# Three pairs of groups instead of two in each feed-forward stage of a two-block transformer kernel

## What is computed

```
def swiglu_ffn(h, w_gate, w_up, w_down):
    return (jax.nn.silu(h @ w_gate) * (h @ w_up)) @ w_down

for layer in range(DEPTH):          # DEPTH = 2
    ...
    h = rmsnorm(x, norm_ffn_g[layer])
    x = x + swiglu_ffn(h, ffn_w_gate[layer], ffn_w_up[layer], ffn_w_down[layer])
```

## Time and profile before

| | |
|---|---|
| median of 3 runs | 716.3 us (716.2 to 716.61) |
| the profiled execution's own time | 715.99 us |
| its span, first to last instruction | 714.1 us |
| TensorE matmul busy | 701.0 us, 98% |
| VectorE busy | 586.1 us, 82% |
| ScalarE busy | 422.6 us, 59% |
| granted TensorE clock, mean | 0.993 of full |

### The profile page before, as it was taken

The page is one execution under the profiler, slowest core; times in us unless marked ns, Lnnn a source line. Parts: engine busy times, 40 slices in busy tenths (PEclk is TensorE's granted clock), DMA queues, the critical chain, the costliest instruction groups (busy, mean ns, idle before and its releaser), DMA issues.

```text
span 714.1 us, 9602 instructions
## 1 busy us (share of the span) xinstructions
PE 701.0 (98%) x3764; PEld 609.7 (85%) x3764; DVE 586.1 (82%) x879; ACT 422.6 (59%) x640; POOL 12.4 (2%) x18
## 2 busy tenths in 40 slices
PE   7999999999999999999999999999999999999996
PEld 6888889989999999888788888888888888888885
DVE  5879999798976889988889688875698896888744
ACT  3156535974775768778845546364667455463623
POOL 0000000000220001000000000000000000000000
PEclk8999999999999999999999999999999999999998
DMA  8999996499935338534704860776345047607501
GB/s 333 417 421 417 422 405 268 175 378 345 391 119 212 145 128 264 138 119 177 265 31 148 324 235 1 307 282 235 119 178 214 22 156 315 236 0 295 176 1 60
DMA packets 23469, 158.41 MB, mean 222 GB/s; under 512 B 2624, under 2 KB 2880, under 8 KB 5248
## 3 DMA queue, kind: packets, MB, share of 16 engines
q1 hardware_dynamic: 22464, 152.82, 55.4%
q0 software_dynamic: 960, 4.98, 2.6%
HBM read 156.74 MB, written 1.05 MB: 221 GB/s over the span
## 4 chain that ended last, share of the span: by engine, by line
PE 80%; DVE 11%; ACT 7%; issue 1%; DMA 1%; SPq 0%; DVEq 0%
PE pb L1909 19%; PE pb L1911 19%; PE pb L1910 19%; PE pb L1981 14%; DVE w L1238 4%; DVE raw L1241 3%; PE pb L2228 2%; PE pb L2333 1%; ACT w L796 1%; PE pb L2451 1%; DMA x<-x_dram 1%; ACT t L914 1%; DVE f L1238 1%; ACT r L911 1%; DVE r L1238 1%
## 5 line engine op out<-in xcount | busy, mean ns | idle before, releaser
L1238 DVE TENSOR_TENSOR w<-raw,w 128x2048 fp32r<-128x2048 f32 x91 | 206.9, 2285 | 55.0 <-ACT w L796 55.0
L796 ACT ACTIVATE w<-raw 128x2048 fp32r<-128x2048 f32 x95 | 179.3, 1911 | 59.2 <-PE pb L1911 29.4
L1909 PE MATMUL pb<-w,r 128*128 128x512 f32 (+1 forms) x528 | 207.2, 392 | 1.7 <-DVE t L1241 1.4
L1911 PE MATMUL pb<-w,r 128*128 128x512 f32 (+1 forms) x528 | 204.2, 387 | 0.0
L1910 PE MATMUL pb<-w,r 128*128 128x512 f32 (+1 forms) x528 | 203.9, 386 | 0.0
L1909 PEld LDWEIGHTS pb<-w,r 128*128 128x128 f32 x528 | 99.2, 188 | 23.4 <-issue 2.0
L1911 PEld LDWEIGHTS pb<-w,r 128*128 128x128 f32 x528 | 99.1, 188 | 20.5
L1910 PEld LDWEIGHTS pb<-w,r 128*128 128x128 f32 x528 | 99.3, 188 | 19.1
L1909 PE MATMUL pb<-r,w 128*128 128x256 f32 x288 | 82.5, 287 | 0.3 <-DVE r L1238 0.3
L1911 PE MATMUL pb<-r,w 128*128 128x256 f32 x288 | 81.5, 283 | 0.0
L1910 PE MATMUL pb<-r,w 128*128 128x256 f32 x288 | 81.5, 283 | 0.0
(11 more groups left out here) (232 smaller groups left out, 916.2 us busy)
## 6 DMA issues: line engine op xcount, KB each, us to landing
raw<-w_dram SPq DMA_DIRECT2D x125, 1024.0 KB, 6.2
ow<-w_dram SPq DMA_DIRECT2D x8, 1024.0 KB, 16.2
ow<-w_dram SPq DMA_DIRECT2D x8, 512.0 KB, 16.8
f<-w_dram SPq DMA_DIRECT2D x4, 1024.0 KB, 7.6
oh<-w_dram SPq DMA_DIRECT2D x2, 1024.0 KB, 23.6
w<-w_dram POOLq DMA_DIRECT2D x2, 1024.0 KB, 14.8
x<-x_dram SPq DMA_DIRECT2D x2, 512.0 KB, 5.6
acc<-row_dram POOLq DMA_DIRECT2D x2, 512.0 KB, 3.9
```

The source lines that it names most:

```text
L796: return e.activation(out, in_, ACT.Copy, **kw)
L1238: return e.tensor_tensor(out, a, b, op)
L1909: e.matmul(out, a_hi, b_hi, start=start, stop=False)
L1911: return e.matmul(out, a_lo, b_hi, start=False, stop=stop)
```

## The change

`PAIRS` goes from two to three entries, so the units become 0, 1, 2, (3, 4), 5, (6, 7), 8, (9, 10), and the last unit of a stage is a pair. The first sum of a pair is made after the low part of slab 21 instead of after that of slab 11. ScalarE's stream in a pair has the high parts of the coming slabs ahead of silus. VectorE's stream in a pair has `t` ahead of a low part, and in the last pair the low part of the slab three ahead after the last `hidden` instead of in the middle.

```
-PAIRS = (3, 7)
+PAIRS = (3, 6, 9)
...
                         snap(layer, i)
                         fill(k + 1)
                         fill(k + 2)
+                        fill(k + 3)
                         gates(layer, i, [0])
                         hidden_high(layer, i - 1)
-                        fill(k + 3)
                         fill(k + 4)
                         fill(k + 5)
+                        fill(k + 6)
                         gates(layer, i + 1, [1])
-                        fill(k + 6)
+                        fill(k + 7)
                         gates(layer, i + 1, [0])
-                        fill(k + 7)
                         gates(layer, i, [1])
                         fill(k + 8)
...
-                    if PLAN[i][0] in ("11", "form"):
+                    if PLAN[i][0] in ("21", "form"):
                         form_sums(k, *PLAN[i])
...
-                if kind == "11":
+                if kind == "21":
                     top = part(layer, 0, g)
                     p.wait_ge(*landed(top))
-                    p.wait_ge(s_lo, LOW_AT[k])
+                    p.wait_ge(s_lo, LOW_AT[AT["11", layer, g]])
                     tt_(chain, chain, raw_of(top)[:, :], ADD).then_inc(s_form, 1)
...
                         hidden_low(layer, i - 1)
                         fill(k + 3)
                         made_from(layer, i, "u2", "c11")
+                        made_from(layer, i, "t", "u2")
                         fill(k + 4)
-                        made_from(layer, i, "t", "u2")
                         fill(k + 5)
                         made_from(layer, i, "u3", "t")
                         made_from(layer, i, "c22", "t")
                         fill(k + 6)
                         hidden(layer, i + 1, [1])
                         made_from(layer, i, "c12", "c22")
-                        fill(k + 7)
+                        if i + 2 < NG:
+                            fill(k + 7)
                         hidden(layer, i + 1, [0])
                         made_from(layer, i, "c21", "u3")
                         hidden(layer, i, [1])
+                        fill(k + 7)
                         fill(k + 8)
```

## The result

The changed kernel takes 720.65 us (median of 4 runs, 719.7 to 722.01) against 716.25 us (4 runs, 715.84 to 716.61). The ratio is 1.0063, 95% interval 1.0048 to 1.0079. The forecast was 719.3 us.

A forecast was written before the change was run, and what follows sets the result against it. TensorE was taken as the bound, with VectorE perhaps not keeping up. From 715.99 us, 6.8 saved against 8.1 of waits gave 717.3, median 717.6; the clock's 1.7 made 719.3 us, range 716.0 to 722.3.

The forecast's parts named there:

- 24 matmuls fewer: TensorE in the feed-forward stages: a third pair per stage saves 12 matmuls per layer, 5.4 us in all.
- the small waits after pairs: TensorE's 0.3 us wait around the first down product after a pair goes, four times, 1.2 us.
- A pair overdraws VectorE and the ordinary group behind it pays back: A pair costs VectorE 35.0 us against TensorE's 30.4; the following group recovers the 4.6 us, but the last pair has none.
- The last half is ready 31.3 us after product 11, TensorE wants it at 27.9: Last pair's half (9, 1), before the transposes: TensorE waits 3.4 us in each layer.
- Second wait of 1.5 us in layer 0 only: TensorE waits 1.5 us for group 9's `hidden_low` behind two slabs' low parts in layer 0; nothing in layer 1.
- The sum without the clock, +1.3 us: Both layers together: 6.8 us saved on TensorE against 8.1 us of new waits, giving a median of 717.6 us.
- The clock costs 1.7 us in layer 1 and is hidden in layer 0: TensorE's clock falls after the 3.4 us waits, adding 1.7 us in layer 1; layer 0's second wait hides it.
- Moving the first sum costs 1 us: Moving it behind slab 21 costs about 1 us of VectorE's lead over product 11 of the last pair.
- The signs: Two waits of about 3 us, one of 1.2 to 1.5, 24 fewer matmuls, VectorE near 100% busy, clock at 0.50.
- The two pieces of 0.5 us: TensorE's small waits, 0.5 us in two pieces, were taken for waits after pairs and should be gone.

The follow-up runs named there:

- orders_alone: The changed kernel's new orders with the pairs (3, 4) and (7, 8) of before: 714.95 us against 716.43 for the kernel before.
- last_halves_first: Changed kernel; in the last pair VectorE's hidden halves precede down 9's low part, transposed groups precede down 10's, ScalarE likewise: 709.77 us against 716.43 before.
- two_pairs_adjacent: The changed kernel's new orders with only the pairs (3, 4) and (6, 7): 714.95 us, ratio 0.998 to the kernel before.
- one_more_vector_op: Changed kernel plus an unused VectorE maximum over 2048 columns before hidden (10, 0) of the last pair: 724.12 us against 716.24 before.
- vector_order_alone: VectorE's last-pair order with hidden halves first, but ScalarE's fills at the changed kernel's places: 712.11 us against 716.04 for the kernel before.
- filled_wait: Changed kernel plus 12 unused matmuls on TensorE inside the last pair's long wait before the transposes: 719.08 us against 716.24 before.
- first_sum_early: Changed kernel with a pair's first sum back behind the low part of slab 11 instead of slab 21: 717.97 us against 716.24 before.
- pairs_alone: Kernel before with three pairs, PAIRS = (3, 6, 9), and nothing else changed: 746.68 us, ratio 1.0426.
- down_9_behind: Changed kernel with only down 9's low part in the last pair moved behind the last hidden half: 722.93 us against 716.24 before.
- pair_not_last: Changed kernel with the pairs (2, 3), (5, 6), (8, 9), so group 10 follows as an ordinary group: 728.12 us against 716.04 before.

## Why the prediction held, point by point

- **24 matmuls fewer are worth 5.4 us, and the small waits after pairs 1.2 us.** Right within 0.4 us. orders_alone gives 1.2 to 1.5 us. last_halves_first, which has no wait at the end, is 6.7 us faster than before between medians, against 6.8; by starts of the same instructions it is 3.2 us in each layer (194.68 against 197.90 us from layer 0's first transposes to layer 1's, 154.75 against 157.98 from there to the last matmul), where the forecast has 3.4.
- **A pair overdraws VectorE and the ordinary group behind it pays back.** Right for pair (6, 7): two_pairs_adjacent shows no wait.
- **The last half is ready 31.3 us after product 11, TensorE wants it at 27.9.** Right: 31.4 us, waits of 3.3 us in both layers. one_more_vector_op (1.5 us of 2.2), vector_order_alone (1.0 of 1.2) and last_halves_first (no wait left) move it by the expected order of size.
- **Second wait of 1.5 us in layer 0 only.** Right, 1.47 us.
- **The sum without the clock, +1.3 us.** Too small, and in part a slip: the prediction's own waits, 3.4 + 3.4 + 1.5, are 8.3 and not 8.1, which gives +1.5. The two stages give +1.9 and about +0.1 us, 2.0 together. Two errors make up the rest: TensorE's gain is 3.2 us per layer and not 3.4, and a wait costs a little more than its idle time, since the first matmuls after it are slower. By starts of matmuls, against last_halves_first, the three waits cost 3.4, 1.7 and 3.4 us.
- **The clock costs 1.7 us in layer 1 and is hidden in layer 0.** The mechanism was forecast, the size was luck. The 1.7 was the middle between nothing and 3.4 us, taken for a reason that no run tests (how loaded TensorE is as it resumes). In the profiled execution the clock is at half for 3.4 us in layer 1, which costs 1.7; in layer 0 it didn't fall, though the wait there is as long, and nothing in the prediction tells the two layers apart. filled_wait shows that the fall goes with the idle wait and that its cost is real, 1.6 us. The hiding in layer 0 was seen in first_sum_early.
- **Moving the first sum costs 1 us.** 1.2 us per layer in the changed kernel. Its old place costs nothing after a pair in the new orders (first_sum_early); in the orders of before it puts 2.2 us of VectorE's time ahead of `hidden_low` (pairs_alone), but whether the wait would go without it was not run.
- **The signs.** The two long waits, the third, the 24 matmuls and the clock came as named. Two signs did not. The two pieces of 0.5 us stayed, because they never were the waits after pairs. And VectorE is not near 100% busy in the wait itself: between 494.4 and 497.5 us it is 63% busy, since it stands twice for a silu that ScalarE can start only after VectorE's own c12 or c21; over the whole stretch from e to the last half it is 94% busy.
- **The size, 719.3 against 720.65.** For the profiled execution the forecast comes to 719.0 (715.99 + 1.3 + 1.7), and it took 720.06. Of these 1.1 us, 0.7 are the sum above, 0.2 were there before any changed code, and 0.1 lies behind the last matmul. The stretch ahead of the stages differs by up to 1 us from execution to execution: the same instruction starts at 319.8, 320.0 and 320.7 us in the traces of before, after and filled_wait. The last 0.3 us is that this execution lies 0.6 us below its median, where that of before lies 0.3 below; it is not explained.

One thing stays open. The runs of the changed kernel reach from 719.7 to 722.01 us, and the slowest has a mean clock of 0.993, no lower than the others (0.990 to 0.992). That this spread comes with the idle waits is not shown. It is 0.6 us in 5 runs when the wait is filled and 0.7 us in 4 runs without it, but the kernel before, which has no such wait, spreads over 2.2 us in one of its sessions (7 runs). How a single run gets to 722 isn't known, as its trace was not at hand. Nor were the moves of `t` and of ScalarE's other high parts tried one by one.

## What to carry to other kernels

Work that an engine does ahead of time is free only while something stands behind it that pays it back; look at the last unit of each stage by itself. When a result closes a stage, put everything it needs at the front of each engine's stream, and the preparation of later slabs behind it: here only the places of a few instructions separated +0.6% from -0.9%. Move the preparation on all engines at once, since a wait that is removed on one stream shows up at the next instruction that was behind it (down_9_behind).

## What was not expected of the hardware

TensorE with twelve more useless matmuls per layer was faster than TensorE idle: the wait of 3.3 us in layer 1 costs another 1.6 to 1.7 us by the clock (1.2 instead of 2.4 GHz) after the work has resumed. The clock did not fall after every such wait (layer 0 of the changed kernel, 3.3 us idle, stayed at 1.00), but did after one of 2.1 us (first_sum_early). In pair_not_last it fell about 2.3 us into an idle stretch of 8.2 us and came back 10.2 us later, 4.4 us after TensorE had resumed. Over all the traces of the stages, the clock fell in or right after every wait of 3.7 us or more (seven), after one of the two of 3.3 us in the changed kernel, in or after two of the seven of 2.1 to 2.6 us, and after none of 1.6 us or less. Equal waits of one execution went both ways: the two of 3.3 us in the changed kernel, and the two of 2.1 us in first_sum_early.
